# Feed-forward of the second block: 1/rms applied to the product instead of to the tokens, first weight unit split in quarters

## The chip, the cores and the metric

The kernel runs on one core of a Trainium2 chip. The metric is the device time of one launch in microseconds. TensorE (PE) multiplies into PSUM, VectorE (DVE) and ScalarE (ACT) do the elementwise work, GpSimd (POOL) adds some squares, and SyncE (SP) starts the loads of weights from HBM.

## The reference

The whole model is two blocks of two layers each. The first block is a conditioned trunk, the second a plain one, and the change is only in the second:

```
def rms_norm_2(x, g, eps=NORM_EPS):
    xf = x.astype(jnp.float32)
    y = xf * lax.rsqrt(jnp.mean(xf * xf, axis=-1, keepdims=True) + eps)
    return (y * g.astype(jnp.float32)).astype(x.dtype)

def swiglu_2(x, w_gu, w_down):
    g, u = jnp.split(x @ w_gu, 2, axis=-1)
    return (jax.nn.silu(g) * u) @ w_down

    for l in range(DEPTH):
        x = x + 0.5 * swiglu_2(rms_norm_2(x, ffn1_norm[l]), ffn1_w_gu[l], ffn1_w_down[l])
        x = x + hybrid_mixer(rms_norm_2(x, mix_norm[l]), ...)
        x = x + 0.5 * swiglu_2(rms_norm_2(x, ffn2_norm[l]), ffn2_w_gu[l], ffn2_w_down[l])
```

There are 256 tokens, `x` has 1024 features, the hidden width is 2816, everything is float32. The feed-forward half stands four times in the second block.

## The kernel before

Tokens lie along the free axis and features along the 128 partitions: `x` is 8 chunks of 128 x 256, the hidden layer 22 chunks, of which 11 are kept at a time. All weights come in units through a ring of four slots (`weights0` to `weights3`); a plan (`weight_plan`) fixes the order of units for the whole program. SP loads unit n + 4 when TensorE has reported unit n done (`unit_done`), whatever stage it belongs to.

A product in full precision is made of three passes on parts in fp32r: high x high, high x low, low x high (`product_of_parts`, L484 in the profile). So each weight unit is split before use: ScalarE copies the 2048 columns into the high part (`split_high`, L460), VectorE subtracts it from the original to give the low part (`split_low`, L468). There are four buffers of such parts for the second block, and the splits of unit q + 4 are issued right after the eviction of unit q, on the same two engines.

`half_ffn` (L913) does one feed-forward half as four products in a row: "in a" (11 units), "out a" (8 units), "in b" (11), "out b" (8). An "in" unit holds one gate tile and one up tile of 128 columns, 2 x 8 x 3 = 48 products of 128x128 by 256 tokens. An "out" unit holds 11 x 3 = 33. An "out" unit multiplies all 11 chunks of hidden, and the first one of each half waits chunk by chunk for them (`banks_free`).

The opening of `half_ffn`: two products with a matrix of ones sum the squares over the partitions (`sum_over_chunks`, L411 and L413), ScalarE takes the root (L942), VectorE the reciprocal (L1020), then chunk by chunk VectorE scales `x` by gain and 1/rms (L1027), ScalarE copies the high part (L949) and VectorE subtracts the low part (L1039). TensorE starts the first unit chunk by chunk behind these. The other three splits of the first four units follow after the chunks on VectorE.

In the body the two engines work on an "in" unit in this manner (ScalarE, then VectorE):

```
nc.scalar.activation(row[:, T], k.psum[:, 2 * slot, T], ACT.Silu).then_inc(t["silu_done"].sem, 1)
act.wait_ge(t["gated"].sem, i * RING + (t["gated"].base + n))
nc.scalar.activation(one(k.hidden[0], i * RING + c, col=T), row[:, T], ACT.Copy)\
    .then_inc(t["hidden_high"].sem, 1)
split_high(act, i, at(spec, c) + depth)
...
nc.vector.tensor_tensor(row, row, k.psum[:, 2 * slot + 1, T], ALU.mult).then_inc(t["gated"].sem, 1)
dve.wait_ge(t["hidden_high"].sem, i * RING + (t["hidden_high"].base + n))
nc.vector.tensor_tensor(one(k.hidden[1], i * RING + c, col=T), row,
                        one(k.hidden[0], i * RING + c, col=T).bitcast(F32), ALU.subtract)\
    .then_inc(k.banks_free, 1)
split_low(dve, i, at(spec, c) + depth)
```

These are L962 and L964 on ScalarE, L1051 and L1053 on VectorE. The 11 "in" units are run as two turns of a hardware loop of four and three unrolled ones. Every block ends and begins with a barrier of all engines.

Of the kernel before, what the change touches and what calls it, by code (L numbers as in the profile page):

```python
# [13 lines left out]
P = 128  # L14
# [171 lines left out]
def pair_tiles(slot):  # L186

    return slot[:, 0:2 * KD * P].rearrange("p (t k c) -> p t k c", t=2, k=KD)
# [171 lines left out]
def one(t, h, rows=slice(None), col=slice(None)):  # L360

    if isinstance(h, int):
        return t[rows, h, col]
    return t[rows, bass.ds(h, 1), col].rearrange("p o n -> p (o n)")
# [6 lines left out]
def square_buffers(k, tokens):  # L371

    T = slice(0, tokens)
    return k.square[:, 0, T], [k.square[:, 1, T], k.rinvs[:, 1, T]]
# [11 lines left out]
def sum_squares(k, block, tokens):  # L386

    squared, summed = k.tally("x_squared"), k.tally("x_summed")
    total, buffers = square_buffers(k, tokens)
    first, done = squared.base, summed.base  # L390

    @block.gpsimd
    def _(pool):
        for n in range(1, KD - 1):
            pool.wait_ge(squared.sem, first + n + 1)
            if n > 1:
                pool.wait_ge(summed.sem, done + n - 1)
            k.nc.gpsimd.tensor_tensor(total, total, buffers[n % 2], ALU.add).then_inc(summed.sem, 1)  # L398


def close_squares(k):
    k.tally("x_squared").close(KD)
    k.tally("x_summed").close(KD - 2)


def sum_over_chunks(k, pe, tokens):

    squared, summed = k.tally("x_squared"), k.tally("x_summed")
    total, buffers = square_buffers(k, tokens)
    pe.wait_ge(summed.sem, summed.base)  # L410
    k.nc.tensor.matmul(k.psum[:, 0, 0:tokens], k.const("ones"), total, start=True, stop=False)  # L411
    pe.wait_ge(squared.sem, squared.base)
    return k.nc.tensor.matmul(k.psum[:, 0, 0:tokens], k.const("ones"), buffers[(KD - 1) % 2], start=False, stop=True)  # L413


def prepare_sqrt(k):

    k.nc.scalar.activation(k.spare[:, 0:1], k.eps[:, 0:1], ACT.Sqrt)
# [23 lines left out]
def weight_parts(k, specs, depth):  # L442


    nc, first, total = k.nc, specs[0].start, sum(s.n for s in specs)
    per_unit = 16 * specs[0].dmas[0]
    ready = [r for s in specs for r in s.ready]
    high, low = k.tally("high_done"), k.tally("split_done")
    high_before, low_before = high.base, low.base

    def split_high(act, i, q):

        if q >= total:
            return
        slot, part = (first + q) % RING, (first + q) % depth
        act.wait_ge(k.weights_ready[slot], i * per_unit + ready[q])

        if first + q >= depth:
            act.wait_ge(k.unit_done, i * RING + (first + q - depth + 1))
        nc.scalar.activation(k.parts[part][0][:, :], k.slots[slot][:, 0:WIDE], ACT.Copy).then_inc(high.sem, 1)  # L460

    def split_low(dve, i, q):

        if q >= total:
            return
        slot, part = (first + q) % RING, (first + q) % depth
        dve.wait_ge(high.sem, i * RING + (high_before + q + 1))
        nc.vector.tensor_tensor(k.parts[part][1][:, :], k.slots[slot][:, 0:WIDE], k.parts[part][0][:, :].bitcast(F32),  # L468
                                ALU.subtract).then_inc(low.sem, 1)

    def wait_parts(pe, i, q):

        pe.wait_ge(low.sem, i * RING + (low_before + q + 1))
        pe.wait_ge(k.banks_free, i * RING + (first + q + 1))
        return (first + q) % RING, k.parts[(first + q) % depth]

    high.close(total), low.close(total)
    return split_high, split_low, wait_parts
# [424 lines left out]
def ffn_buffers(k, tokens, depth):  # L903

    stack, sb = scoped(k, F32R)
    k.normed = [sb(f"normed{n}", [P, KD, tokens]) for n in range(2)]
    k.hidden = [sb(f"hidden{n}", [P, KH, tokens]) for n in range(2)]
    part_buffers(k, sb, depth)
    k.rows = [k.roots[:, 1, 0:tokens], k.rinvs[:, 1, 0:tokens]]
    return stack  # L910


def half_ffn(k, tokens, name, layer, gain, shift, gate):  # L913
# [155 lines left out]
                each_unit(dve, 0, spec.n, unit_in if s % 2 == 0 else unit_out, s < len(specs) - 1)  # L1069
    for name, n in dict(summed=1, root_done=1, inverse_done=1, scaled=KD, shifted=KD, normed=KD,  # L1070
                        silu_done=KF, gated=KF, hidden_high=KF).items():
        t[name].close(n)
    close_squares(k)

# [1154 lines left out]
def second_block(k, w):  # L2229
    k.cos2, k.sin2 = k.r_stage[0:ROPE2, 0, :], k.r_stage[0:ROPE2, 1, :]  # L2230
    k.selector = w["selector"].rearrange("j (h t) -> j h t", h=4)
    rope_tables(k)
    for l in (0, 1):
        for m in ("ffn1", "mix", "ffn2"):
            at_gain = k.vec_at[f"{m}_b{l}"]
            gain = lambda c, cond, at_gain=at_gain: column(k.vec, at_gain + c)
            if m == "mix":
                hybrid_mixer(k, l, gain)
            else:
                half_ffn(k, LAT, m, f"_b{l}", gain, None, 0.5)  # L2240

# [107 lines left out]
```

## Time and profile before

| what | value |
|---|---|
| device time, median of 3 runs | 4143.72 us (4138.34 to 4143.89) |
| profiled execution, its own time | 4139.52 us |
| span of the profiled execution | 4137.5 us |
| mean granted TensorE clock | 0.937 of full speed |
| TensorE busy | 3673.6 us (89%) |
| VectorE busy | 2044.2 us (49%) |
| ScalarE busy | 1511.6 us (37%) |
| GpSimd busy | 251.5 us (6%) |
| read from HBM | 474.65 MB |

The second block runs from about 2345 us to the end; its four feed-forward halves open at 2345.2, 3028.7, 3232.8 and 3919.2 us. Times in the tables are from the start of the span. A timeline row gives start, length, engine, line, operation, what it writes and reads, the number of instructions merged, and in square brackets how long the engine was idle before it and what ended that. The clock column of the windows tells the share of full speed that TensorE was granted: 1.0 is 2.4 GHz, 0.5 is 1.2 GHz.

### The profile page before, as it was taken

The numbers are of one execution on the slowest core, as the hardware profiler recorded it, in microseconds if no ns is written. First come the engines' busy times: TensorE is split into PE (matmuls) and PEld (weight loads), VectorE is DVE, ScalarE is ACT, GpSimd is POOL, SyncE is SP. The second block draws the span as 40 slices with busy tenths as digits, with TensorE's granted clock in tenths as the row PEclk, the third lists the DMA queues.
The fourth block names the chain that finished last, engine by engine and source line by source line (L and its number), as shares of the span: only waits on it lengthen the run. The fifth ranks groups of instructions, "written<-read, shape, count | busy, mean of one in ns | idle before, by whom it ended". The sixth has DMA issues, their size and how long they took to land. (4 is left out here: it accounts for less than half of the span.)

```text
span 4137.5 us, 57956 instructions
## 1 busy us (share of the span) xinstructions
PE 3673.6 (89%) x22018; PEld 3096.7 (75%) x22018; DVE 2044.2 (49%) x2625; ACT 1511.6 (37%) x1840; POOL 251.5 (6%) x169
## 2 busy tenths in 40 slices
PE   7899987788999999988889898967989998768898
PEld 5688842367887678866579898945989998648898
DVE  5733347444335843331455555455455555554455
ACT  3522311233223532221244544334344444253343
POOL 0000010100001000020100001010000001200000
PEclk9999998899999999999899999988999999878999
DMA  7633330013334923342026565501646565204464
GB/s 259 208 83 109 87 77 32 21 31 82 96 86 151 296 78 100 84 104 81 1 81 179 148 180 156 159 1 30 171 134 180 163 177 171 79 0 104 138 172 134
DMA packets 807728, 478.13 MB, mean 116 GB/s; under 512 B 33413, under 2 KB 806004, under 8 KB 807428
## 3 DMA queue, kind: packets, MB, share of 16 engines
q1 hardware_dynamic: 797200, 473.13, 40.2%
q10 hardware_dynamic: 10356, 2.63, 0.4%
q8 instruction: 118, 1.93, 0.2%
q14 instruction: 54, 0.44, 0.0%
HBM read 474.65 MB, written 1.05 MB: 115 GB/s over the span
## 5 line engine op out<-in xcount | busy, mean ns | idle before, releaser
L484 PE MATMUL psum<-normed,weights_part 128*128 128x256 f32 (+1 forms) x11232 | 1728.8, 316 | 87.5 <-DVE normed L1041 28.6
L484 PEld LDWEIGHTS psum<-normed,weights_part 128*128 128x128 f32 x11232 | 1583.5, 192 | 226.8 <-issue 82.4
L468 DVE TENSOR_TENSOR weights_part<-weights,weights_part 128x2048 fp32r<-128x2048 f32 x460 | 1052.9, 2292 | 799.9 <-ACT weights_part L460 799.5
L460 ACT ACTIVATE weights_part<-weights 128x2048 fp32r<-128x2048 f32 x460 | 878.1, 1912 | 841.9 <-PE psum L484 340.7
L484 PE MATMUL psum<-hidden,weights_part 128*128 128x256 f32 (+1 forms) x4224 | 681.0, 323 | 11.1 <-DVE hidden L1053 11.1
L484 PEld LDWEIGHTS psum<-hidden,weights_part 128*128 128x128 f32 x4224 | 615.4, 190 | 74.8 <-DVE hidden L1053 13.1
L398 POOL TENSOR_TENSOR square<-square,rinvs 128x256 f32<-128x256 f32 (+1 forms) x39 | 70.2, 1799 | 2675.1 <-ACT rinvs L383 2672.9
L484 PE MATMUL psum<-weights_part,cond_part 128*2 128x256 f32 x1728 | 216.5, 281 | 12.1 <-DVE weights_part L468 12.1
L484 PEld LDWEIGHTS psum<-weights_part,cond_part 128*2 128x2 f32 x1728 | 138.9, 83 | 70.2 <-issue 12.9
L1051 DVE TENSOR_TENSOR rinvs<-rinvs,psum 128x256 f32<-128x256 f32 (+1 forms) x88 | 45.5, 517 | 174.4 <-ACT rinvs L962 174.4
L1063 DVE SCALAR_TENSOR_TENSOR x<-psum,gate,x 128x256 f32 (+1 forms) x112 | 49.7, 479 | 163.5 <-PE psum L484 163.4
L1051 DVE TENSOR_TENSOR roots<-roots,psum 128x256 f32<-128x256 f32 (+1 forms) x88 | 45.5, 517 | 169.6 <-ACT roots L962 169.6
L962 ACT ACTIVATE rinvs<-psum 128x256 f32<-128x256 f32 (+1 forms) x88 | 39.8, 453 | 229.6 <-PE psum L484 229.6
L846 DVE TENSOR_REDUCE negmax<-psum 128x1 f32<-128x256 f32 (+1 forms) x128 | 66.8, 524 | 91.2 <-PE psum L2160 18.9
L1337 PE MATMUL psum<-h,weights 128*128 128x512 f32 (+1 forms) x224 | 98.4, 602 | 13.3 <-PEq L494 13.3
L962 ACT ACTIVATE roots<-psum 128x256 f32<-128x256 f32 (+1 forms) x88 | 40.0, 455 | 188.4 <-PE psum L484 188.2
L964 ACT ACTIVATE hidden<-rinvs 128x256 f32 (+3 forms) x88 | 43.8, 498 | 165.4 <-DVE rinvs L1051 165.4
L964 ACT ACTIVATE hidden<-roots 128x256 f32 (+3 forms) x88 | 43.8, 498 | 156.5 <-DVE roots L1051 156.5
L1337 PEld LDWEIGHTS psum<-h,weights 128*128 128x128 f32 (+1 forms) x224 | 41.9, 188 | 69.7 <-issue 69.7
L2152 PE MATMUL psum<-heads,q_stage 128*128 128x256 f32 (+1 forms) x128 | 46.6, 451 | 42.2 <-POOL q_stage L786 42.2
L484 PE MATMUL psum<-mixed_part,weights_part 128*128 128x512 f32 (+1 forms) x384 | 71.6, 352 | 11.4 <-DVE mixed_part L585 11.4
L1053 DVE TENSOR_TENSOR hidden<-rinvs,hidden 128x256 f32 (+3 forms) x88 | 46.3, 526 | 64.8 <-ACT hidden L964 64.8
(297 smaller groups left out, 3163.8 us busy)
## 6 DMA issues: line engine op xcount, KB each, us to landing
weights<-in_l_ffn_w_in SPq DMA_DIRECT2D x176, 512.0 KB, 5.1
weights<-in_ffn_w_gu SPq DMA_DIRECT2D x176, 512.0 KB, 5.1
weights<-in_l_mod_w SPq DMA_DIRECT2D x72, 1024.0 KB, 5.1
weights<-in_w_in SPq DMA_DIRECT2D x34, 1024.0 KB, 5.2
weights<-in_w_gate SPq DMA_DIRECT2D x64, 512.0 KB, 4.7
weights<-in_l_ffn_w_out SPq DMA_DIRECT2D x64, 384.0 KB, 4.1
weights<-in_ffn_w_down SPq DMA_DIRECT2D x64, 384.0 KB, 4.1
weights<-in_l_ffn_w_out SPq DMA_DIRECT2D x64, 320.0 KB, 3.4
```

Of the source, the lines that this page charges most:

```text
L398: k.nc.gpsimd.tensor_tensor(total, total, buffers[n % 2], ALU.add).then_inc(summed.sem, 1)
L460: nc.scalar.activation(k.parts[part][0][:, :], k.slots[slot][:, 0:WIDE], ACT.Copy).then_inc(high.sem, 1)
L468: nc.vector.tensor_tensor(k.parts[part][1][:, :], k.slots[slot][:, 0:WIDE], k.parts[part][0][:, :].bitcast(F32), ALU.subtract).then_inc(lo ...
L484: mm = k.nc.tensor.matmul(to, left[a], right[b], start=first and n == 0, stop=last and n == len(PASSES) - 1)
L846: nc.vector.tensor_reduce(k.negmax[:, j:j + 1], S[j], AX.X, ALU.max, negate=True).then_inc(t["maxed"].sem, 1)
L962: nc.scalar.activation(row[:, T], k.psum[:, 2 * slot, T], ACT.Silu).then_inc(t["silu_done"].sem, 1)
L964: nc.scalar.activation(one(k.hidden[0], i * RING + c, col=T), row[:, T], ACT.Copy)\
L1051: nc.vector.tensor_tensor(row, row, k.psum[:, 2 * slot + 1, T], ALU.mult).then_inc(t["gated"].sem, 1)
L1053: nc.vector.tensor_tensor(one(k.hidden[1], i * RING + c, col=T), row, one(k.hidden[0], i * RING + c, col=T).bitcast(F32), ALU.subtract)\
L1063: last = nc.vector.scalar_tensor_tensor(row, k.psum[:, 2 * slot, part], gate(chunk, cond) if callable(gate) else gate, row, ALU.mult, ALU.add)
L1337: mm = nc.tensor.matmul(k.psum[0:m, 2 * slot + t, :], lhs, k.h[:, kc, :], start=kc == 0, stop=kc == KD - 1)
L2152: return nc.tensor.matmul(ps, k.q_stage[:, hh, qt * P:(qt + 1) * P], one(k.heads, key_head), start=True, stop=last)
```

## The change

In the second block `half_ffn` is replaced by `late_ffn`. The tokens that are multiplied are `x` times the gain only. The factor 1/rms is the same for all features of a token, so it is applied to the gate and the up product when they leave PSUM, as two multiplications on VectorE, and Silu then reads the scaled gate in SBUF. The sum of squares is taken by TensorE after the first unit, in a bank of the fourth unit, which waits until the root has been read. The first unit's two splits are cut in four quarters (two feature chunks of both tiles each) and alternate with the parts of the tokens.

```
-def sum_over_chunks(k, pe, tokens):
+def sum_over_chunks(k, pe, tokens, bank=None):
...
+    bank = k.psum[:, 0, 0:tokens] if bank is None else bank
...
+        @block.scalar
+        def _(act):
+            act.wait_ge(k.weights_ready[first % RING], specs[0].ready[0])
+            for p in range(pieces):
+                last = nc.scalar.activation(piece(part0[0], p), piece(slot0, p), ACT.Copy)
+                last.then_inc(t["piece_high"].sem, 1)
+                for c in range(p * per, (p + 1) * per):
+                    nc.scalar.activation(k.normed[0][:, c, T], k.x[:, c, T], ACT.Copy, scale=gain(c, 0))\
+                        .then_inc(t["source_high"].sem, 1)
+            act.sem_inc(high.sem, 1)
+            split_high(act, 0, 1)
+            split_high(act, 0, 2)
+
+            act.wait_ge(t["summed"].sem, t["summed"].base + 1)
+            nc.scalar.activation(k.root[:, T], norm_bank, ACT.Sqrt, bias=k.eps[:, 0:1], scale=1.0 / D)\
+                .then_inc(t["root_done"].sem, 1)
+            split_high(act, 0, 3)
...
+                    act.wait_ge(t["scaled"].sem, i * RING + (t["scaled"].base + n))
+                    nc.scalar.activation(g, g, ACT.Silu).then_inc(t["silu_done"].sem, 1)
+                    act.wait_ge(t["gated"].sem, i * RING + (t["gated"].base + n))
+                    nc.scalar.activation(one(k.hidden[0], i * RING + c, col=T), g, ACT.Copy)\
+                        .then_inc(t["hidden_high"].sem, 1)
+                    split_high(act, i, at(spec, c) + depth)
...
+                if s == 0:
+                    slot = first % RING
+                    pe.wait_ge(k.banks_free, first + 1)
+                    for kc in range(KD):
+                        pe.wait_ge(t["piece_low"].sem, t["piece_low"].base + kc // per + 1)
+                        pe.wait_ge(t["normed"].sem, t["normed"].base + kc + 1)
+                        for tile in range(2):
+                            mm = product_of_parts(k, k.psum[:, 2 * slot + tile, T], [pair_tiles(w)[:, tile, kc] for w in part0],
+                                                  [x[:, kc, T] for x in k.normed], kc == 0, kc == KD - 1)
+                    mm.then_inc(k.unit_done, 1)
+
+                    sum_over_chunks(k, pe, tokens, norm_bank).then_inc(t["summed"].sem, 1)
+                    each_unit(pe, 1, 3, unit_in)
+                    pe.wait_ge(t["root_done"].sem, t["root_done"].base + 1)
+                    each_unit(pe, 3, spec.n, unit_in)
...
+            for p in range(pieces):
+                dve.wait_ge(t["piece_high"].sem, t["piece_high"].base + p + 1)
+                nc.vector.tensor_tensor(piece(part0[1], p), piece(slot0, p), piece(part0[0], p).bitcast(F32), ALU.subtract)\
+                    .then_inc(t["piece_low"].sem, 1)
+                for c in range(p * per, (p + 1) * per):
+                    dve.wait_ge(t["source_high"].sem, t["source_high"].base + c + 1)
+                    nc.vector.scalar_tensor_tensor(k.normed[1][:, c, T], k.x[:, c, T], gain(c, 0),
+                                                   k.normed[0][:, c, T].bitcast(F32), ALU.mult, ALU.subtract)\
+                        .then_inc(t["normed"].sem, 1)
+            dve.sem_inc(low.sem, 1)
+            split_low(dve, 0, 1)
+            split_low(dve, 0, 2)
+            dve.wait_ge(t["root_done"].sem, t["root_done"].base + 1)
+            nc.vector.reciprocal(k.rinv[:, T], k.root[:, T]).then_inc(t["inverse_done"].sem, 1)
+            split_low(dve, 0, 3)
...
+                    nc.vector.tensor_tensor(g, k.psum[:, 2 * slot, T], k.rinv[:, T], ALU.mult).then_inc(t["scaled"].sem, 1)
+                    nc.vector.tensor_tensor(u, k.psum[:, 2 * slot + 1, T], k.rinv[:, T], ALU.mult).then_inc(t["upper"].sem, 1)
+                    dve.wait_ge(t["upper"].sem, i * RING + (t["upper"].base + n))
+                    dve.wait_ge(t["silu_done"].sem, i * RING + (t["silu_done"].base + n))
+                    nc.vector.tensor_tensor(g, g, u, ALU.mult).then_inc(t["gated"].sem, 1)
+                    dve.wait_ge(t["hidden_high"].sem, i * RING + (t["hidden_high"].base + n))
+                    nc.vector.tensor_tensor(one(k.hidden[1], i * RING + c, col=T), g,
+                                            one(k.hidden[0], i * RING + c, col=T).bitcast(F32), ALU.subtract)\
+                        .then_inc(k.banks_free, 1)
+                    split_low(dve, i, at(spec, c) + depth)
...
-                half_ffn(k, LAT, m, f"_b{l}", gain, None, 0.5)
+                late_ffn(k, m, f"_b{l}", gain, 0.5)
```

How the instructions stand on an engine. TensorE at the opening of a half in the second block, before (L484 are the weight products, `weights_part_2_14` is a part of the first unit, `weights_part_3_14` of the second):

```order
L978 UNCONDITIONAL_BRANCH [waits barrier_Pool_Activation_PE_DVE_SP_release]
L411 MATMUL psum<-square,consts 128x256 [waits x_summed]
L413 MATMUL psum<-rinvs,consts 128x256 [waits x_squared]
L484 MATMUL psum<-normed_14,weights_part_2_14 128x256 [waits ffn_normed,banks_free,split_done]
L484 MATMUL psum<-normed_14,weights_part_2_14 128x256 x5
...
L484 MATMUL psum<-normed_14,weights_part_3_14 128x256 [waits banks_free,split_done]
```

and now:

```order
L1148 UNCONDITIONAL_BRANCH [waits barrier_Pool_Activation_PE_DVE_SP_release]
L485 MATMUL psum<-normed_14,weights_part_2_14 128x256 [waits late_normed,late_piece_low,banks_free]
L485 MATMUL psum<-normed_14,weights_part_2_14 128x256 x5
...
L412 MATMUL psum<-square,consts 128x256 [waits x_summed]
L414 MATMUL psum<-rinvs,consts 128x256 [waits x_squared]
L485 MATMUL psum<-normed_14,weights_part_3_14 128x256 [waits banks_free,split_done]
```

The two sum products moved from ahead of the first unit to behind it.

VectorE at the same opening, up to the first eviction, before:

```order
L468 TENSOR_TENSOR weights_part_2_14<-weights,weights_part_2_14 128x2048 [waits high_done]
L1020 RECIPROCAL rinvs<-roots 128x256 [waits ffn_root_done]
L1027 SCALAR_TENSOR_TENSOR roots<-x,vec,rinvs 128x256 [waits ffn_inverse_done]
L1027 SCALAR_TENSOR_TENSOR rinvs<-x,vec,rinvs 128x256
L1039 TENSOR_TENSOR normed_14<-roots,normed_14 128x256 [waits ffn_shifted]
...
L468 TENSOR_TENSOR weights_part_3_14<-weights,weights_part_3_14 128x2048 [waits high_done]
L468 TENSOR_TENSOR weights_part_0_14<-weights,weights_part_0_14 128x2048 [waits high_done]
L468 TENSOR_TENSOR weights_part_1_14<-weights,weights_part_1_14 128x2048 [waits high_done]
```

and now:

```order
L1193 TENSOR_TENSOR weights_part_2_14<-weights,weights_part_2_14 128x2x256 [waits late_piece_high]
L1197 SCALAR_TENSOR_TENSOR normed_14<-x,vec,normed_14 128x256 [waits late_source_high] x2
...
L469 TENSOR_TENSOR weights_part_3_14<-weights,weights_part_3_14 128x2048 [waits high_done]
L469 TENSOR_TENSOR weights_part_0_14<-weights,weights_part_0_14 128x2048 [waits high_done]
L1204 RECIPROCAL rinvs<-roots 128x256 [waits late_root_done]
L469 TENSOR_TENSOR weights_part_1_14<-weights,weights_part_1_14 128x2048 [waits high_done]
```

The reciprocal moved from the second place to between the third and the fourth unit's split, and the whole split of the first unit became quarters (the first two rows stand four times).

VectorE in the loop over "in" units, one unit, before:

```order
L1050 REGISTER_ALU [waits unit_done]
L1051 TENSOR_TENSOR roots<-roots,psum 128x256 [waits ffn_silu_done]
L1053 ISA [waits ffn_hidden_high]
L1053 TENSOR_TENSOR hidden_14<-roots,hidden_14 128x256
L467 REGISTER_ALU
L468 TENSOR_TENSOR weights_part_2_14<-weights,weights_part_2_14 128x2048 [waits high_done]
```

and now:

```order
L1212 REGISTER_ALU [waits unit_done]
L1213 TENSOR_TENSOR roots<-psum,rinvs 128x256 [waits banks_free]
L1214 TENSOR_TENSOR roots<-psum,rinvs 128x256
L1215 REGISTER_ALU
L1217 TENSOR_TENSOR roots<-roots 128x256 [waits late_silu_done,late_upper]
L1219 ISA [waits late_hidden_high]
L1219 TENSOR_TENSOR hidden_14<-roots,hidden_14 128x256
L468 REGISTER_ALU
L469 TENSOR_TENSOR weights_part_2_14<-weights,weights_part_2_14 128x2048 [waits high_done]
```

Two scalings came in ahead of the product of the two halves; Silu on ScalarE (L1132) now waits for the first of them (`late_scaled`) where it waited for the unit itself.

## Rows read from the trace of the kernel before

**Rows 1.** Page, part 1, TensorE: busy us (share of the span), instructions.

```profile
PE 3673.6 (89%) x22018; PEld 3096.7 (75%) x22018; DVE 2044.2 (49%) x2625; ACT 1511.6 (37%) x1840; POOL 251.5 (6%) x169
```

**Rows 2.** Windows, all engines, second half-FFN: busy (count), clock, DMA share, GB/s.

```profile
3036.00:3229.00 193.00, 190.14 (x1567) 189.56 (x1568) 111.70 (x110) 92.32 (x98) 9.78 (x6) 0.99 0.61 170
```

**Rows 3.** Timeline of TensorE, opening and turns: start, length, merged count [idle before].

```profile
3028.70 0.83 PE L411 MATMUL psum<-square,consts 128*128 128x256 f32 x2 [2.39 <-PEq L548]
3029.33 1.06 PE L413 MATMUL psum<-rinvs,consts 128*128 128x256 f32 x2
3036.21 7.35 PE L484 MATMUL psum<-normed,weights_part 128*128 128x256 f32 x48 [5.82 <-DVE normed L1039]
3044.03 16.21 PE L484 MATMUL psum<-normed,weights_part 128*128 128x256 f32 x133 [0.47 <-DVE weights_part L468]
...
3101.72 3.76 PE L484 MATMUL psum<-hidden,weights_part 128*128 128x256 f32 x30
3106.40 5.77 PE L484 MATMUL psum<-hidden,weights_part 128*128 128x256 f32 x46 [0.92 <-DVE hidden L1053]
...
3197.93 3.76 PE L484 MATMUL psum<-hidden,weights_part 128*128 128x256 f32 x30
3202.95 1.21 PE L484 MATMUL psum<-hidden,weights_part 128*128 128x256 f32 x8 [1.26 <-DVE hidden L1053]
```

**Rows 4.** Timeline of VectorE, one unit of the loop.

```profile
3087.28 2.29 DVE L468 TENSOR_TENSOR weights_part<-weights,weights_part 128x2048 fp32r<-128x2048 f32 x1 [1.25 <-ACT weights_part L460]
3089.49 0.41 DVE L1051 TENSOR_TENSOR rinvs<-rinvs,psum 128x256 f32<-128x256 f32 x1
3090.62 0.43 DVE L1053 TENSOR_TENSOR hidden<-rinvs,hidden 128x256 f32 x1 [0.72 <-ACT hidden L964]
3092.29 2.29 DVE L468 TENSOR_TENSOR weights_part<-weights,weights_part 128x2048 fp32r<-128x2048 f32 x1 [1.25 <-ACT weights_part L460]
```

**Rows 5.** Timeline of ScalarE, the same unit.

```profile
3090.04 0.42 ACT L964 ACTIVATE hidden<-rinvs 128x256 f32 x1 [2.52 <-DVE rinvs L1051]
3090.36 1.90 ACT L460 ACTIVATE weights_part<-weights 128x2048 fp32r<-128x2048 f32 x1
```

**Rows 6.** Timeline of VectorE, last unit before a turn, first after, last two.

```profile
3105.02 0.41 DVE L1051 TENSOR_TENSOR roots<-roots,psum 128x256 f32<-128x256 f32 x1
3105.92 0.42 DVE L1053 TENSOR_TENSOR hidden<-roots,hidden 128x256 fp32r<-128x256 f32 x1 [0.48 <-ACT hidden L964]
...
3145.37 0.41 DVE L1051 TENSOR_TENSOR rinvs<-rinvs,psum 128x256 f32<-128x256 f32 x1
...
3196.67 0.41 DVE L1051 TENSOR_TENSOR roots<-roots,psum 128x256 f32<-128x256 f32 x1
...
3201.58 0.41 DVE L1051 TENSOR_TENSOR rinvs<-rinvs,psum 128x256 f32<-128x256 f32 x1
```

**Rows 7.** Timeline of VectorE, the reciprocal at the opening.

```profile
3032.89 1.75 DVE L1020 RECIPROCAL rinvs<-roots 128x256 f32<-128x256 f32 x1
```

**Rows 8.** Timeline of ScalarE: 512 columns, and 256 columns with a bias operand.

```profile
160.04 0.63 ACT L383 ACTIVATE rinvs<-x 128x512 f32<-128x512 f32 x1 [1.93 <-POOL square L398]
...
2344.44 0.49 ACT L1719 ACTIVATE r_stage<-roots,half_pi 16x256 f32<-16x256 f32 x1
```

**Rows 9.** Windows, TensorE alone: busy (count), clock; gaps and what follows them.

```profile
2101.10:2106.70 5.60, 0.04 (x1) 0.77 0.00 0
2106.70:2110.90 4.20, 4.20 (x20) 0.50 0.00 0
...
2862.30:2867.50 5.20, 0.06 (x2) 0.78 0.00 0
2867.50:2872.10 4.60, 4.60 (x21) 0.50 0.00 0
...
3030.00:3036.00 6.00, 0.39 (x1) 0.50 0.24 59
3060.00:3100.00 40.00, 40.00 (x336) 1.00 0.59 164
```

More of the change, by code:

```diff
@@ L403, in close_squares @@
     k.tally("x_summed").close(KD - 2)
-def sum_over_chunks(k, pe, tokens):
+def sum_over_chunks(k, pe, tokens, bank=None):
     squared, summed = k.tally("x_squared"), k.tally("x_summed")
     total, buffers = square_buffers(k, tokens)
+    bank = k.psum[:, 0, 0:tokens] if bank is None else bank
     pe.wait_ge(summed.sem, summed.base)
-    k.nc.tensor.matmul(k.psum[:, 0, 0:tokens], k.const("ones"), total, start=True, stop=False)
+    k.nc.tensor.matmul(bank, k.const("ones"), total, start=True, stop=False)
     pe.wait_ge(squared.sem, squared.base)
-    return k.nc.tensor.matmul(k.psum[:, 0, 0:tokens], k.const("ones"), buffers[(KD - 1) % 2], start=False, stop=True)
+    return k.nc.tensor.matmul(bank, k.const("ones"), buffers[(KD - 1) % 2], start=False, stop=True)
 def prepare_sqrt(k):
```

75 lines of the change are left out of this document (added).

## The prediction

> **What bounds the kernel now.** I read the page's head first: TensorE is busy for 89% of the span [rows 1], so nothing is gained except where TensorE waits or is slow. The change touches only the four feed-forward halves of the second block (FFN below). Their body from first to last product is seen in one stretch of the engines' windows: TensorE is busy 190.14 of 193.00 us, VectorE 111.70, ScalarE 92.32, DMA 0.61 [rows 2]. So the body is TensorE's. From 3106.40 to 3197.93 it issues 762 products (3 + 7 x 33 + 11 x 48) in 91.5 us, 0.120 us each: a unit "in" takes 5.77 us (ten take 57.7 from 3044.03 to 3101.72), a unit "out" 3.96 [rows 3]. It waits at three places: at the opening (block starts at 3028.70, first product at 3036.21, second unit at 3044.03, thus 15.3 us), and at each turn from "in" to "out", where chunk 10 of hidden is awaited: 0.92 and 1.26 us [rows 3].
>
> Next the timelines of VectorE and ScalarE, for what follows TensorE in the body. One round of the two runs in series: low split starts 3087.28, silu x up 3089.49, high part of hidden 3090.04, high split 3090.36, next low split 3092.29. That is 2.21 + 0.55 + 0.32 + 1.93 = 5.01 us [rows 4, 5], 4.91 in the unrolled last three units (3196.67 to 3201.58, [rows 6]). TensorE needs 5.77, so this ring has 0.76 us in hand per round; this is what I hold the change against.
>
> **The change part by part.** *Opening.* Before, VectorE does the low split of unit 0, the reciprocal (1.75 us, [rows 7]), eight scalings and eight parts, and then three low splits at 2.21 each. After, by ScalarE: a quarter of 512 columns takes 0.63 us as the square of 512 does, 0.53 start to start [rows 8]; the two gain copies carry a pointer as the sine with its bias, 0.49, thus 0.40 start to start [rows 8]. Four rounds take 4 x (0.53 + 0.80) = 5.3 us, high split 1 ends at 7.2 and 2 at 9.0 (all from the block's start). VectorE: a low quarter is 0.15 + 512 x 1.045 ns = 0.69, two subtractions at 0.43 each: 4 x (0.60 + 0.86) = 5.9, begun at 0.75, done at 6.6. Low split 1 runs 7.25 to 9.45, 2 to 11.65. TensorE can start at about 2.0. The clock was already at the half in the idle stretch before (0.50 from 3030 to 3036, [rows 9]), and I take it to be so still. Some 5 us of its first unit may run at 0.215 us per product: unit 0 ends between 8.5 and 10.1. The two sum products take 1.7 us at the half clock (3028.70 to 3030.39, [rows 3]) and some 1.1 at the full one, so the second unit starts at 9.6 to 11.5, I take 10.5, against 15.3. TensorE thus leaves the opening 4.8 us earlier.
>
> *But VectorE does not.* Behind low split 2 stands the reciprocal (root at 11.7 at the latest, 1.75 more: 13.4), then low split 3 (2.2, awaiting the high split behind the root): the first eviction starts at 15.6 to 16.2, I take 15.9. TensorE ended that unit at about 10, so VectorE enters the loop some 6 us late. The order below shows why: three whole splits and the reciprocal are still ahead of the loop. The Silu table load falls into ScalarE's idle time.
>
> *Body.* Each of the 22 "in" units per FFN gets a scaling of the gate product on VectorE ahead of Silu, one of the up product beside Silu, and Silu can no longer run while VectorE is in its low split: it waits for the scaling. The ring grows by scaling-to-Silu and Silu-to-product. The nearest handovers are silu x up to high part and high part to low part: 0.45 + 0.45 unrolled (3105.02, then 3105.92, [rows 6]), 0.55 + 0.58 in the loop (3089.49, 3090.04, 3090.62, [rows 4, 5]). In the order, the loop's longer ones have an ISA row between, and the new ones have none, so I take 0.92: ring 5.93 in the loop, 5.83 unrolled. Bounds: +0.90 and +1.13, ring 5.91 to 6.14. Nothing of it can be below zero, because both new steps stand in series. The up scaling (0.41) hides beside Silu. So the ring becomes longer than TensorE's 5.77 and its lag grows by 0.16 per unit, 0.06 unrolled. The four part buffers hold TensorE off this lag: it never waits for a split. But at the turn it needs chunk 10 of hidden at once.
>
> The Trainium skill (VectorE: DVE Perf Modes, the TRN2 errata section) gives cycle sums per instruction: 120 + 256 cycles at 0.96 GHz and 224 + 256 at 1.2, thus an estimate of 0.39 + 0.40 = 0.79, ring 5.80. By that the ring would almost keep up with TensorE. The rows' own durations agree (0.41, 0.42), but the rows also show 0.04 to 0.16 us of handover at each step, so I hold to 5.93.
>
> *First turn.* Chunk 10's eviction starts at 15.9 + 8 x 5.93 + 2 x 5.83 = 75.0. Before, the step from silu x up to TensorE took 1.38 (3105.02 to 3106.40), now 0.90 more: TensorE goes on at 77.3, against 77.7 before (3106.40 less 3028.70). Gain 0.4: the whole opening's gain is spent waiting here. TensorE would be ready at 10.5 + 57.7 + 3.8 = 72.0, so it stands for 5.3 us.
>
> *Second turn.* The opening does not reach here; eight "out" units lie between, in which the ring (2.7 us per unit on VectorE) is shorter than TensorE's 3.96. Before, the first product of silu x up stands at 3145.37. TensorE ended that unit at 3106.40 + 282 x 0.120 = 3140.3, a lag of 5.1, which the arrival of weights sets and which stays. After ten rounds it is 5.1 + 8 x 0.16 + 2 x 0.06 = 6.5, plus 0.90 + 1.38 = 8.8. Before: 3202.95 less 3197.93 = 5.0. Loss 3.8; TensorE stands for 5.0 instead of 1.26.
>
> *Clock.* The gaps of 5.6 us from 2101.1 and 5.2 from 2862.3 were each followed by the half clock (1.2 of 2.4 GHz) for 4.2 and 4.6 us of busy TensorE: 20 and 21 products where the full clock does 336 in 40 us [rows 9]. Per gap that costs 4.4 x (1 - 0.120/0.215) = 1.9 us. The waits of 0.92 and 1.26 brought none. The two new ones are as long as those gaps: 3.9 us per FFN. The page TensorE: Matmul & The Clock Gate of the Trainium skill (section What's actually happening) calls the ramp under 1% of a span and not worth modelling; by that the sum would lose this term, 15.6 of 29 us. I keep it, as the rows price it.
>
> *Sum.* Per FFN -0.4 + 3.8 + 3.9 = 7.3; four of them 29 us. The profiled execution took 4139.52 (span 4137.5 and 2 around it), 4.2 below the median of 4143.72, so 4168.7 for it and **4173** for the median. SP's loads await the same units as before and gain at most a microsecond of lead; DMA is at 0.61 and hides them. The rest of the program is unchanged.
>
> **Rivals.** A difference under 0.2% (8.3 us) I call the same.
> (a) *No half clock after the turns* (the waits fall into it only partly). For it: the ends are near the shortest gaps that I have. Against: both rows above. 4143.7 + 4 x 3.4 = 4157.
> (b) *Longer ring*, 6.14: first turn 15.9 + 61.2 + 2.5 = 79.6, +1.9; second 5.1 + 8 x 0.37 + 2 x 0.27 = 8.6, +2.5 = 11.1, +6.1; with the clock 11.9 per FFN: 4191. For it: the loop's handovers are the long ones. Against: no ISA row at the new ones.
> (c) *The ring just keeps up* (5.80 or less): first turn -1.7, second +2.5, and stalls of about 4 us, half of which bring the low clock: +1 to +4 per FFN, 4148 to 4160; at its lower end no measurable change.
> (d) *Faster*: the opening's 4.8 us go through. It needs VectorE's first eviction by 11 after the block's start, thus its three low splits out of the way, and a ring under 5.77; then 4 x 4.8 = 19 us: 4125. Speaking for it are the four buffers, which do carry TensorE; against it the turn, where no buffer helps. It decides at a chunk 10 evicted by 72.
>
> **Chances.** Forecast 0.50; (a) 0.15; (b) 0.17; (c) 0.11, a third of it as the same; (d) 0.07. The range takes (a) and most of (b): 4150 to 4189. Faster 0.07, same 0.08 (part of (c), and an opening a little better), slower 0.85.
>
> **What would show it.** Second unit at 10 to 11 us after the block's start; first eviction at 15.9; start to start of gate scalings 5.9 in the body; TensorE waits of about 5 us before chunk 10 at both turns, eight in all, ended by VectorE's low part of hidden; granted clock 0.5 behind each. I am wrong if the scalings come every 5.77, if those waits stay near 1 us, or if TensorE stands elsewhere, for a split.

## The result and the profile after

| | median us | runs | ratio to before, 95% interval |
|---|---|---|---|
| before | 4141.03 | 4137.60 to 4143.89 | |
| the change | 4165.05 | 4162.92 to 4168.41 | 1.0059, 1.0042 to 1.0077 |
| the change, taken again with the second set of experiments | 4172.20 | 4164.38 to 4175.84 | 1.0073, 1.0059 to 1.0086 |

The kernel became slower by 24 us (0.6%), and by 32 when it was measured again, against a before of 4139.81 in that set. The forecast was 4173, slower.

The first lines that tell it stand on the page, in its list of the costliest groups: TensorE's products for the "out" units. A row gives the count, the busy time, the mean of one, and the idle time in front with what ended most of it. Before:

```profile
L484 PE MATMUL psum<-hidden,weights_part 128*128 128x256 f32 (+1 forms) x4224 | 681.0, 323 | 11.1 <-DVE hidden L1053 11.1
```

After:

```profile
L485 PE MATMUL psum<-hidden,weights_part 128*128 128x256 f32 (+1 forms) x4224 | 697.4, 328 | 46.3 <-DVE hidden L1219 44.2
```

The same 4224 products wait 35 us more, on hidden, and are 16 us slower (the count has those of the first block too, whose code is the same). Both belong to the turns from "in" to "out" units. TensorE's timeline of the second half (before: [rows 3]; start, length, merged count, idle before):

```profile
3031.84 8.32 PE L485 MATMUL psum<-normed,weights_part 128*128 128x256 f32 x48 [4.26 <-DVE normed L1197]
3040.01 0.59 PE L412 MATMUL psum<-square,consts 128*128 128x256 f32 x2
3040.44 0.59 PE L414 MATMUL psum<-rinvs,consts 128*128 128x256 f32 x2
3040.68 23.50 PE L485 MATMUL psum<-normed,weights_part 128*128 128x256 f32 x193
...
3107.67 4.64 PE L485 MATMUL psum<-hidden,weights_part 128*128 128x256 f32 x20 [5.26 <-DVE hidden L1219]
...
3201.20 3.83 PE L485 MATMUL psum<-hidden,weights_part 128*128 128x256 f32 x30
3210.30 30.23 PE L485 MATMUL psum<-hidden,weights_part 128*128 128x256 f32 x234 [5.27 <-DVE hidden L1219]
```

The block starts here at 3029.95 (ScalarE's first quarter, below). The first product comes 1.9 us after it (before: 7.5), the second unit 10.7 (before: 15.3). But TensorE goes on past the first turn 77.7 us after the start, to the tenth the same as before. At the second turn the "out" products begin at 3201.20 and the first one on chunk 10 comes at 3210.30, 9.1 us later, where it was 5.0. In all eight turns the wait for chunk 10 is 5.26 or 5.27 us. In three of them (at 3313.68, 3417.04 and 4109.95) TensorE also waits 0.58 to 0.81 us for chunk 9.

VectorE at the opening, and one unit of the loop (before: [rows 4, 6, 7]):

```profile
3041.58 1.75 DVE L1204 RECIPROCAL rinvs<-roots 128x256 f32<-128x256 f32 x1
3043.37 2.29 DVE L469 TENSOR_TENSOR weights_part<-weights,weights_part 128x2048 fp32r<-128x2048 f32 x1
3045.58 0.42 DVE L1213 TENSOR_TENSOR roots<-psum,rinvs 128x256 f32<-128x256 f32 x1
...
3055.36 2.29 DVE L469 TENSOR_TENSOR weights_part<-weights,weights_part 128x2048 fp32r<-128x2048 f32 x1 [1.25 <-ACT weights_part L461]
3057.57 0.42 DVE L1213 TENSOR_TENSOR roots<-psum,rinvs 128x256 f32<-128x256 f32 x1
3057.91 0.41 DVE L1214 TENSOR_TENSOR roots<-psum,rinvs 128x256 f32<-128x256 f32 x1
3058.54 0.43 DVE L1217 TENSOR_TENSOR roots<-roots 128x256 f32<-128x256 f32 x1 [0.22 <-ACT roots L1132]
3059.69 0.43 DVE L1219 TENSOR_TENSOR hidden<-roots,hidden 128x256 f32 x1 [0.72 <-ACT hidden L1134]
3061.36 2.29 DVE L469 TENSOR_TENSOR weights_part<-weights,weights_part 128x2048 fp32r<-128x2048 f32 x1 [1.25 <-ACT weights_part L461]
```

and ScalarE, the block's start and the same unit:

```profile
3029.95 0.63 ACT L1114 ACTIVATE weights_part<-weights 128x512 fp32r<-128x512 f32 x1 [0.82 <-PEq L549]
3030.48 0.89 ACT L1117 ACTIVATE normed<-x,vec 128x256 fp32r<-128x256 f32 x2
...
3058.02 0.42 ACT L1132 ACTIVATE roots<-roots 128x256 f32<-128x256 f32 x1 [2.69 <-DVE roots L1213]
3059.11 0.42 ACT L1134 ACTIVATE hidden<-roots 128x256 f32 x1 [0.67 <-DVE roots L1217]
```

From low split to low split it is 6.00 us (3055.36 to 3061.36), where it was 5.01. The 88 "in" units make 80 such rounds, taken here from scaling to scaling: 63 of the 64 in the loop take 5.98 to 6.01 us (one takes 6.14), the 16 unrolled ones 5.88 to 5.90. So even a time is the sign of a ring that waits for nothing outside; before, the same rounds took from 4.91 to 7.27 us. From the scaling to the product of gate and up it is 0.97 (3057.57 to 3058.54), the added part. The up scaling ends at 3058.32, ahead of Silu's end at 3058.44: it costs nothing.

The clock behind the two turns, by windows of TensorE (busy, count, clock):

```profile
3102.40:3107.70 5.30, 0.04 (x2) 0.78 0.03 8
3107.70:3112.20 4.50, 4.50 (x21) 0.50 0.48 142
3112.20:3117.00 4.80, 4.80 (x42) 1.00 0.32 94
...
3210.30:3214.60 4.30, 4.29 (x20) 0.50 0.42 126
```

Behind these two turns TensorE works for 4.5 and 4.3 us at 1.2 GHz, then at 2.4 again; behind the eight it is 3.3 to 5.1 us. Hence 234 products take 30.23 us behind the second turn instead of the 28.33 of before: 1.9 us.

### The profile page after: what moved, and what is told of

Read it like the earlier page. It is cut to its first block and busy times, and to the rows that moved or that the text cites. A ratio compares the mean times of both kernels' runs of the same rounds, so it can differ in the third digit from the quotient of the medians.

```text
span 4160.9 us, 58156 instructions
## 1 busy us (share of the span) xinstructions
PE 3681.6 (88%) x22018; PEld 3108.2 (75%) x22018; DVE 2095.8 (50%) x2781; ACT 1517.2 (36%) x1852; POOL 252.8 (6%) x169
## 5 line engine op out<-in xcount | busy, mean ns | idle before, releaser
L485 PE MATMUL psum<-hidden,weights_part 128*128 128x256 f32 (+1 forms) x4224 | 697.4, 328 | 46.3 <-DVE hidden L1219 44.2
L485 PEld LDWEIGHTS psum<-hidden,weights_part 128*128 128x128 f32 x4224 | 630.7, 195 | 111.1 <-DVE hidden L1219 46.4
L1052 DVE TENSOR_TENSOR rinvs<-rinvs,psum 128x512 f32<-128x512 f32 (+1 forms) x44 | 27.2, 619 | 174.9 <-ACT rinvs L963 174.9
L1052 DVE TENSOR_TENSOR roots<-roots,psum 128x512 f32<-128x512 f32 (+1 forms) x44 | 27.2, 619 | 169.2 <-ACT roots L963 169.2
L963 ACT ACTIVATE rinvs<-psum 128x512 f32<-128x512 f32 (+1 forms) x44 | 23.8, 541 | 230.1 <-PE psum L485 230.1
L963 ACT ACTIVATE roots<-psum 128x512 f32<-128x512 f32 (+1 forms) x44 | 23.8, 542 | 188.3 <-PE psum L485 188.2
L485 PEld LDWEIGHTS psum<-mixed_part,weights_part 128*128 128x128 f32 x384 | 62.8, 202 | 20.0 <-DVE weights_part L469 11.8
L1762 PE MATMUL psum<-h,weights 128*128 128x256 f32 (+1 forms) x208 | 65.2, 476 | 13.3 <-PEq L495 13.3
L735 PE MATMUL psum<-heads,consts 128*128 x132 | 49.2, 529 | 24.4 <-DVE square L753 16.5
```

What stands on the lines that cost most here:

```text
L485: mm = k.nc.tensor.matmul(to, left[a], right[b], start=first and n == 0, stop=last and n == len(PASSES) - 1)
L735: mm = k.nc.tensor.matmul(k.psum[:, u, g * LAT:(g + 1) * LAT], turn, one(src, i * 2 + g, R, N), start=True, stop=True)
L1762: mm = nc.tensor.matmul(k.psum[:, 2 * slot + t, T], W[:, kc, t * P:(t + 1) * P], k.h[:, kc, T], start=kc == 0, stop=kc == KD - 1)
```

## The experiments

Each median is of 4 to 11 runs. The kernel before, run beside them, had 4138.9 in the first set (the opening alone, the ring alone, the first filling, the scaling ahead) and 4139.8 in the second.

**The opening alone.** Silu reads PSUM and the product of the halves too, as before; the factor 1/rms is left out and the gate made small.

```
-                    act.wait_ge(t["scaled"].sem, i * RING + (t["scaled"].base + n))
-                    nc.scalar.activation(g, g, ACT.Silu).then_inc(t["silu_done"].sem, 1)
+                    nc.scalar.activation(g, k.psum[:, 2 * slot, T], ACT.Silu).then_inc(t["silu_done"].sem, 1)
...
-                    nc.vector.tensor_tensor(g, k.psum[:, 2 * slot, T], k.rinv[:, T], ALU.mult).then_inc(t["scaled"].sem, 1)
-                    nc.vector.tensor_tensor(u, k.psum[:, 2 * slot + 1, T], k.rinv[:, T], ALU.mult).then_inc(t["upper"].sem, 1)
...
-                    nc.vector.tensor_tensor(g, g, u, ALU.mult).then_inc(t["gated"].sem, 1)
+                    nc.vector.tensor_tensor(g, g, k.psum[:, 2 * slot + 1, T], ALU.mult).then_inc(t["gated"].sem, 1)
```

> The opening of the change (unscaled tokens, quarters, sum after the first unit) with the ring of before: Silu reads PSUM, no scaling by 1/rms. It leaves out the factor 1/rms in the second block's feed-forward, with a smaller gate to keep the numbers finite. Theory (the opening gains, the longer ring at the turns loses): the ring is 5.0 us again, both turns wait about 1 us, no half clock behind them, and the opening's 4.3 us (second unit 10.9 us after the block's start against 15.3) reach the end: 4 x 4.3 = 17 us under before, about 4124. Rival (the opening's gain is given back to the loads, which start only when the first unit is done, or to the sum of squares in TensorE's queue): within 4 us of before, about 4141.

Measured: 4117.5 us, ratio 0.9950 (0.9937 to 0.9963), 21 us under before. Its row for the "out" products is that of before again:

```profile
L485 PE MATMUL psum<-hidden,weights_part 128*128 128x256 f32 (+1 forms) x4224 | 681.0, 323 | 10.7 <-DVE hidden L1215 8.7
```

So the opening by itself gains, and the gain reaches the end when nothing at the turns takes it: each half is 4.1 to 5.1 us shorter than before, near the 4.6 by which the second unit starts earlier. The rival of the loads falls.

**The ring alone.** The kernel before with the two scalings in its ring; the tokens are normalized already, so 1/rms comes in twice.

```
+                    nc.vector.tensor_tensor(row, k.psum[:, 2 * slot, T], k.rinv[:, T], ALU.mult).then_inc(t["gate_scaled"].sem, 1)
+                    nc.vector.tensor_tensor(u, k.psum[:, 2 * slot + 1, T], k.rinv[:, T], ALU.mult).then_inc(t["upper"].sem, 1)
...
-                    nc.scalar.activation(row[:, T], k.psum[:, 2 * slot, T], ACT.Silu).then_inc(t["silu_done"].sem, 1)
+                    act.wait_ge(t["gate_scaled"].sem, i * RING + (t["gate_scaled"].base + n))
+                    nc.scalar.activation(row[:, T], row[:, T], ACT.Silu).then_inc(t["silu_done"].sem, 1)
```

> The kernel before with only the two scalings put into its ring (on tokens that are normalized already, so the factor comes in twice). Theory: ring 5.99 us, first eviction 19.6 us after the block's start, chunk 10 at the first turn 81.7 against 77.7 (+4.0), at the second turn +4.1, and 1.9 us of half clock behind each: 11.9 us per half, about 47 in all, 4188. Rival (the slowdown of the change comes from its opening, where the reciprocal and three whole splits stand behind the first unit): the scalings hide, 4141 to 4149.

Measured: 4188.7 us, ratio 1.0118 (1.0104 to 1.0133), 50 us over before. The waits and the slow products are those of the change:

```profile
L484 PE MATMUL psum<-hidden,weights_part 128*128 128x256 f32 (+1 forms) x4224 | 695.5, 327 | 47.2 <-DVE hidden L1223 44.8
```

The two parts of the change add up: -21 and +50 make +29, between the two measurements of both together. By the four halves alone (table at the end of this section) -18.5 and +50.8 make 32.3, where the change has 33.1 and 33.3.

**Filled turns, first attempt.** 24 products to a bank that nobody reads, ahead of the wait for chunk 10:

```
                     for kc in range(KH):
                         if c == 0:
-
+                            if kc == KH - 1:
+                                for n in range(24):
+                                    nc.tensor.matmul(k.psum[:, 2 * slot + 1, T], parts[0][:, 0:P], k.hidden[0][:, 0, T],
+                                                     start=n == 0, stop=n == 23)
                             pe.wait_ge(k.banks_free, spec.start - KH + kc + 1 + RING)
```

> The change with 24 products more per turn, written to a bank that nobody reads, ahead of the wait for chunk 10 (2.9 us of the 5.3 us wait). Theory: the wait ends as before at the same time, but only about 2.4 us of it are idle, the clock stays at 1.0 behind it, and each of eight turns gives back 1.9 us: 15 us under the change, about 4150. Rival (the clock costs nothing here since VectorE sets the pace after the turn too, or it falls all the same): 4165.

Measured: 4178.2 us, ratio 1.0095 (1.0081 to 1.0110). The expectation was wrong, first by the edit: `c == 0` is the body's first place in the loop, so the fill also ran in the fifth "out" unit of each first half, where it costs 2.9 us and hides nothing:

```profile
3105.80 3.04 PE L1165 MATMUL psum<-hidden,weights_part 128*128 128x256 f32 x24
3111.23 17.59 PE L485 MATMUL psum<-hidden,weights_part 128*128 128x256 f32 x132 [2.39 <-DVE hidden L1222]
3128.65 3.04 PE L1165 MATMUL psum<-hidden,weights_part 128*128 128x256 f32 x24
```

And second, the 2.4 us of idle time that were left did not keep the clock: around six of the eight turns it fell all the same, though for 3.4 us instead of 6.8 (of which TensorE was busy 3.2 to 3.4). Behind the turn above:

```profile
3112.40:3115.80 3.40, 3.40 (x18) 0.50 0.73 209
```

The "out" products' busy time is 692.1 us, 6.0 less than in the change (698.1 in its second profile). Four fills in vain of 2.9 us cost 11.7, so the two make the 6 us by which this kernel is over the change's 4172.2.

**Filled turns, once and nearly whole.** 40 products, and the "out" units unrolled on TensorE, so that the fill stands in the first one only:

```
-                    each_unit(pe, 0, spec.n, unit_out, s < len(specs) - 1)
+                    each_unit(pe, 0, spec.n, unit_out, False)
```

> The change with 40 more products per turn to a bank that nobody reads, ahead of the wait for chunk 10, now in the first out unit only (the out units unrolled on TensorE; the fill before also ran in the fifth unit of the loop, 2.9 us each time, and left 2.4 us of the wait idle). They fill 4.8 of 5.3 us. Theory (the half clock behind each turn is due to its idle stretch and costs 1.9 us): no half clock there, the out units after it take 28.3 us instead of 30.2, 15 us under the change, about 4150. Rival (the clock falls for another reason, or its fall costs nothing because VectorE or the loads set the pace): 4165.

Measured: 4158.2 us, ratio 1.0041 (1.0027 to 1.0054); 14.0 us under the change in the same comparison (4172.2), where 15 were expected; the 4150 was counted from the first median, 4165. No turn is followed by the half clock, and the idle time is nearly filled:

```profile
3108.02 4.95 PE L1165 MATMUL psum<-hidden,weights_part 128*128 128x256 f32 x40
3113.45 11.78 PE L485 MATMUL psum<-hidden,weights_part 128*128 128x256 f32 x96 [0.49 <-DVE hidden L1222]
...
L485 PE MATMUL psum<-hidden,weights_part 128*128 128x256 f32 (+1 forms) x4224 | 682.9, 323 | 8.2 <-DVE hidden L1222 6.3
```

The busy time went back from 698.1 (the change, second profile) to 682.9, by 15.2 us or 1.9 per turn. This is the price of the clock, apart from that of the wait. The unrolling was not tried without the fill; as the products' own time gives back 15.2 us, little is left for it.

**Scaling ahead of the split.** One move on VectorE: the scalings of unit q + 1 ahead of the low split of unit q + 4 (and those of the first unit ahead of the fourth's split).

```
-                    nc.vector.tensor_tensor(g, k.psum[:, 2 * slot, T], k.rinv[:, T], ALU.mult).then_inc(t["scaled"].sem, 1)
-                    nc.vector.tensor_tensor(u, k.psum[:, 2 * slot + 1, T], k.rinv[:, T], ALU.mult).then_inc(t["upper"].sem, 1)
                     dve.wait_ge(t["upper"].sem, i * RING + (t["upper"].base + n))
...
                         .then_inc(k.banks_free, 1)
+                    if c + 1 < KH:
+                        scale(spec, half, i, c + 1)
                     split_low(dve, i, at(spec, c) + depth)
```

> The change with one thing moved on VectorE: the two scalings of unit q + 1 stand ahead of the low split of unit q + 4, where VectorE waits for ScalarE anyway, so that Silu runs beside the split. Theory: the ring falls from 5.99 to 5.0 us, TensorE's 5.77 bounds the body again, the turns wait about 1 us, the opening's gain stays: about 4124, under both kernels. Rival (it is the number of operations on VectorE or the PSUM reads that cost, not their place in series): as the change, 4165. Second rival (VectorE now waits for unit q + 1 ahead of a split that TensorE needs, which delays the splits): 4145 or more.

Measured: 4114.9 us, ratio 0.9947 (0.9935 to 0.9960): faster than before by 24 us, faster than the change by some 50. Of the 24 us the four halves give 19.5, near the 17 expected; the rest lies outside them. The same 88 units with the same operations:

```profile
3038.14 0.43 DVE L1224 TENSOR_TENSOR hidden<-roots,hidden 128x256 f32 x1 [0.70 <-ACT hidden L1134]
3038.49 0.42 DVE L1212 TENSOR_TENSOR rinvs<-psum,rinvs 128x256 f32<-128x256 f32 x1
3038.82 0.41 DVE L1213 TENSOR_TENSOR rinvs<-psum,rinvs 128x256 f32<-128x256 f32 x1
3039.86 2.29 DVE L469 TENSOR_TENSOR weights_part<-weights,weights_part 128x2048 fp32r<-128x2048 f32 x1 [0.63 <-ACT weights_part L461]
3042.07 0.42 DVE L1222 TENSOR_TENSOR rinvs<-rinvs 128x256 f32<-128x256 f32 x1
3043.21 0.43 DVE L1224 TENSOR_TENSOR hidden<-rinvs,hidden 128x256 f32 x1 [0.72 <-ACT hidden L1134]
```

The scalings stand where VectorE waited 1.25 us for ScalarE's high split. Of that wait 0.63 is left, and the product of the halves follows the low split at once: hidden to hidden is 5.07 us (3038.14 to 3043.21). The waits for chunk 10 are 0.92 to 1.82 us, and none brings the half clock. It was the place in series that cost, not the number of operations.

**Last chunk first.** At each turn the splits behind the tenth and eleventh "in" unit are put off until chunk 10 is done, on both engines.

```
+    def splits_behind(c):
+        return {KH - 2: [], KH - 1: [KH - 2, KH - 1]}.get(c, [c])
...
-                    split_low(dve, i, at(spec, c) + depth)
+                    for late in splits_behind(c):
+                        split_low(dve, i, at(spec, late) + depth)
```

> The scaling-ahead kernel, and at each turn the splits behind the tenth and eleventh unit are put off until chunk 10 of hidden is done, on both engines. Theory (what is left at the turns is the low split and the high split in front of chunk 10): chunk 10 is ready 2.3 us after its unit, ahead of the 3.8 us at which TensorE wants it, so the eight waits of about 1.1 us go and nothing is late in their place: 9 us under the scaling-ahead kernel (4115), about 4106. Rival (the put-off splits are then late for the third and fourth out unit, or for the next half): 4115 or more.

Measured: **4105.0** us (4104.1 to 4107.2), ratio 0.9915 (0.9901 to 0.9928), 10 us under the one above. The turn is gone from TensorE's timeline, and from its row of "out" products:

```profile
3089.13 11.08 PE L485 MATMUL psum<-hidden,weights_part 128*128 128x256 f32 x91
...
L485 PE MATMUL psum<-hidden,weights_part 128*128 128x256 f32 (+1 forms) x4224 | 678.9, 323 | 2.0 <-DVE hidden L1054 2.0
```

What is left of the wait (2.0 us) is the first block's.

**Whole split of the first unit.** The scaling-ahead kernel with one number changed:

```
-    nc, T, U, tokens, depth, pieces = k.nc, slice(0, LAT), slice(LAT, TOK), LAT, 4, 4
+    nc, T, U, tokens, depth, pieces = k.nc, slice(0, LAT), slice(LAT, TOK), LAT, 4, 1
```

> The scaling-ahead kernel with one number changed, the first unit is split in one piece instead of four. Theory (the opening's gain now reaches the end, since the ring is short): TensorE starts its first product about 4.7 us after the block's start instead of 1.9 and its second unit some 2.3 us later, 4 x 2.3 = 9 us over the scaling-ahead kernel (4115), about 4124. Rival (the quarters bring nothing, since VectorE's whole splits behind them set the second unit): 4115.

Measured: 4130.7 us, ratio 0.9976 (0.9967 to 0.9985), 15.8 over the scaling-ahead kernel's median, which is of the other set of runs; expected were 9. TensorE's first two units, in this kernel and then with quarters:

```profile
3027.26 8.53 PE L485 MATMUL psum<-normed,weights_part 128*128 128x256 f32 x48 [7.14 <-DVE normed L1197]
...
3036.30 15.94 PE L485 MATMUL psum<-normed,weights_part 128*128 128x256 f32 x130
```

```profile
3022.64 8.31 PE L485 MATMUL psum<-normed,weights_part 128*128 128x256 f32 x48 [4.27 <-DVE normed L1197]
...
3031.46 20.74 PE L485 MATMUL psum<-normed,weights_part 128*128 128x256 f32 x170
```

The first product starts 4.8 us after the block's start (3022.49), as expected, but the first unit is no shorter for having its tokens ready: 8.5 against 8.3 us, with the clock at the half for 5.8 us of it here and 5.3 us there. So the second unit is 3.1 us later (13.8 against 10.7), 12 us in four halves. By the table below the four halves are 10.2 us longer than with quarters, so the mechanism expected is confirmed; what the medians show beyond it lies outside the halves, in code that is the same in both. Without the quarters, 10.2 of the 19.5 us go: they are about half of what is gained there.

**The change again.**

> The changed kernel once more, unchanged. Its four halves took 33 us more than before in its first profile, while its median is 24 more, and the first block, whose code is the same, ran 5.5 us shorter in that profile. Theory (that stretch varies from run to run): the halves again 8 us longer each, the first block within 2 us of before, the median 4165 to 4170. Rival (the change shortens the rest of the program in some way): 5 us shorter again in the first block, median 4165.

Measured: 4172.2 us, as in the table; the halves came as expected, the median 2 us over. The stretch that the change touches can be timed in each profile by instructions that are the same in all: from the last GpSimd square ahead of a half to the last one at its end. For the second half, before:

```profile
3027.63 0.72 POOL L398 TENSOR_TENSOR square<-square 128x256 f32<-128x256 f32 x1 [3.92 <-ACT square L383]
...
3228.31 0.73 POOL L398 TENSOR_TENSOR square<-square 128x256 f32<-128x256 f32 x1 [0.89 <-ACT square L383]
```

and in the change:

```profile
3028.90 0.72 POOL L398 TENSOR_TENSOR square<-square 128x256 f32<-128x256 f32 x1 [3.92 <-ACT square L383]
...
3237.57 0.74 POOL L398 TENSOR_TENSOR square<-square 128x256 f32<-128x256 f32 x1 [0.97 <-ACT square L383]
```

That is 200.68 and 208.67 us. All four halves together, and what is left of the span, against the profile of before:

| kernel | four halves, us | rest of the program, us |
|---|---|---|
| the change | +33.1 | -9.7 |
| the change again | +33.3 | +0.9 |
| opening alone | -18.5 | -3.5 |
| ring alone | +50.8 | +2.5 |
| filled turns, first attempt | +39.8 | -6.2 |
| filled turns, once | +17.8 | +0.9 |
| scaling ahead | -19.5 | -6.9 |
| last chunk first | -31.2 | -1.2 |
| whole split | -9.3 | -3.8 |

So the halves agree within 0.2 us in the two profiles of the change, and the rest, whose code is that of before, varies by some 12 us from profile to profile. In the change's first profile 5.6 of the 9.7 us are in the first block, whose start-to-end lies between 5.6 us under and 2.1 over that of before in the nine, without order. The difference between 24 and 32 is in this spread, and the second figure is nearer to what the change does. Why the rest varies was not tried.

## Why the prediction was right

*The opening.* Second unit at 10.5, measured 10.7; the gain of 4.8 was 4.6. Two errors nearly cancel in it: the first unit ended 10.2 us after the start, just outside the 8.5 to 10.1 of the working, and the sum products put only 0.7 us between it and the second unit, not 1.1. The experiment of the opening alone shows that the gain is real. First eviction 15.9 after the start, measured 15.6.

*The ring.* 5.93 and 5.83, measured 5.99 and 5.89. I took the short handover (0.45 + 0.45) and 0.02 more; all 88 units show 0.45 from scaling to Silu and 0.52 or 0.53 from Silu to the product. My reason for the short one, no ISA row in between, holds for the first step only. The rule of the Trainium skill that I weighed (VectorE: DVE Perf Modes, the errata section), with its estimate of 5.80, gave the instructions' own lengths within 0.03 us (0.42 and 0.42) and left out the two handovers, 0.03 and 0.10 us. Rival (c) falls with it.

*First turn.* Forecast -0.4 us, measured 0.0: the ring's 0.06 in ten rounds adds 0.6, the longer step at the end 0.1, and the earlier first eviction takes 0.3 back. *Second turn.* +3.8, measured +4.1, not only by the ring: its ten rounds add some 0.7, but VectorE begins them 4.6 us behind the end of TensorE's first unit (3148.22 against 3137.85 + 5.77) and not 5.1, which takes 0.5 back. So the small error here is partly luck. In both the mechanism and place are as predicted: the wait is for VectorE's low part of chunk 10 (in three turns a little for chunk 9 too), it stands at the eight turns, and behind the openings TensorE waits for no split.

*Clock.* 3.9 us per half, measured 1.9 behind each of eight turns by the filled turns, and 2.0 to 2.1 by the busy time of the "out" products against before. Rival (a) falls. The Trainium skill (TensorE: Matmul & The Clock Gate, What's actually happening) puts the ramp under 1% of a span, and this case agrees: 15 us are 0.4% of 4172. But my reading of it, that the term could then be left out, does not hold here: the difference to be forecast was itself under 1% of the span, and the clock is 15 of its 32 us.

*Sum.* Per half 7.3 predicted; the measured terms make 0.0 + 4.1 + 3.8 = 7.9, or 32 in all, and the halves themselves are 8.0 to 8.8 us longer. So the forecast of 29 was some 4 us short. That 4173 stands within a microsecond of the second median (4172.2) is luck: it was added to a before of 4143.7, which is 4 us over the 4139.8 of that set. In the first comparison, with 24 us, the spread outside the halves hid a part of the loss, as its profile shows (-9.7 in the table above).

*Rival (d)*, the opening's gain going through, was wrong for this kernel but right in its condition: the experiments that shortened the ring got it, and with it a kernel faster than before. My sum took the ring for given with its operations; I did not ask where else on VectorE they could stand.

## What to carry to other kernels

When an operation is moved into a loop that two helper engines run in turns, add its duration and its handovers to that loop's round and compare with the bound engine's; beyond it, the lag grows and is paid where the bound engine next needs the last result; here four buffers in between only moved the payment to the turns. Before giving up such a change, look for the place where the helper waits for the other one: the same two operations moved there turned 24 to 32 us of loss into 24 of gain (in the four halves, 33 of loss into 19.5 of gain). At a turn that waits for the last item, let the helpers finish that item ahead of work that is due later.

## What the runs showed of the hardware

With full work before and behind, waits of 5.25 to 5.27 us on TensorE brought the half clock at all eight turns (the change, in both profiles), waits of 2.4 us at six of eight (filled turns, first attempt), and waits up to 1.82 us at none (scaling ahead). Forty products that nobody reads, put into each of the eight waits, held the clock at 1.0, and the kernel was 14 us faster for them.

The handover from one engine to another, which I had taken as 0.45 us from start to start for 256 columns, is 0.45 from scaling to Silu and 0.52 or 0.53 from Silu to the product in all 88 units of the change. From the product to the high part and from there to the low part it is 0.46 and 0.45 in unrolled units, 0.56 and 0.58 in the loop. Why the steps differ was not tried. These hundredths make the ring 5.99 us instead of the 5.93 forecast, over TensorE's 5.77 in either case.

The time of code that no one touched varied by some 12 us between profiles of one launch each. A change of under 1% is better judged by the stretch that it touches than by the whole.
